# Three z units among the gate steps of a delta stage, its meta recurrence among the merge steps, and the input of the next up-projection rounded from the scaled tiles of a layer norm

## What is computed

```python
proj = h @ w_in                                   # k, q, v, z of 8 heads x 128, and two columns a head
qkv = silu(causal_dwconv(qkv, conv_w))            # then l2norm of q and k
m = where(strict, k_beta @ k.T * decay, 0)        # by chunk and head
a_mat = eye + m                                   # its inverse is applied to v and k
def step(state, inp):                             # over the chunks
    v_new = u_i - w_i @ state
    o_i = qg_i @ state + qk_i @ v_new
    state = state * exp(gl_i) + kd_i.T @ v_new
o = o * rsqrt(mean(o * o) + eps) * norm_w * silu(z)
```

## Time and profile before

| | |
|---|---|
| median of 3 runs | 1368.37 us (1367.38 to 1368.89) |
| the profiled execution | 1367.68 us, its span 1366.0 us |
| TensorE busy | 1298.6 us, 95% of the span |
| DVE, ACT, POOL busy | 1004.5, 688.7 and 45.0 us |
| DMA | 244.62 MB, mean 179 GB/s |
| granted TensorE clock, mean | 0.987 |

### The profile page before, as it was taken

The page is one execution under the profiler, slowest core; times in us unless marked ns, Lnnn a source line. Parts: engine busy times, 40 slices in busy tenths (PEclk is TensorE's granted clock), DMA queues, the critical chain, the costliest instruction groups (busy, mean ns, idle before and its releaser), DMA issues.

```text
span 1366.0 us, 29005 instructions
## 1 busy us (share of the span) xinstructions
PE 1298.6 (95%) x10514; PEld 1274.3 (93%) x10514; DVE 1004.5 (74%) x1811; ACT 688.7 (50%) x1098; POOL 45.0 (3%) x83
## 2 busy tenths in 40 slices
PE   6996999999999999999999799999999999999997
PEld 5995989899999999999999799999998989999997
DVE  6787654899897899899886677774565667777743
ACT  5863533465554354465554355553364554655531
POOL 0001000001001100000000000000000000000000
PEclk9998999999999999999999999999999999999999
DMA  6441002368888868668885346565455334556651
GB/s 222 142 152 47 1 17 78 124 208 292 270 296 288 276 210 296 186 211 289 273 288 172 114 129 184 180 220 184 132 170 177 117 101 141 170 182 182 220 182 40
DMA packets 65351, 244.62 MB, mean 179 GB/s; under 512 B 7264, under 2 KB 9600, under 8 KB 65280
## 3 DMA queue, kind: packets, MB, share of 16 engines
q1 hardware_dynamic: 54624, 204.70, 45.6%
q0 software_dynamic: 10656, 38.93, 9.2%
HBM read 242.56 MB, written 1.05 MB: 178 GB/s over the span
## 4 chain that ended last, share of the span: by engine, by line
PE 74%; DVE 5%; ACT 1%; issue 1%; DVEq 0%; ACTq 0%
PE ps L1582 22%; PE ps L1583 22%; PE ps L1584 22%; PE ps L1597 1%; DVE wlo L374 1%; PE ps L1603 1%; PE ps L1598 1%; PE ps L1963 1%; PE ps L1965 1%; PE ps L1964 1%; DVE xb L1259 1%; DVE xb L1289 1%; PE ps L2075 1%; ACT whi L367 0%; PE ps L2053 0%
## 5 line engine op out<-in xcount | busy, mean ns | idle before, releaser
L1582 PE MATMUL ps<-hhi,whi 128*128 128x258 f32 (+4 forms) x2024 | 578.3, 286 | 9.1 <-DVE small L1491 2.6
L1583 PE MATMUL ps<-hlo,whi 128*128 128x258 f32 (+4 forms) x2024 | 573.9, 284 | 0.0
L1584 PE MATMUL ps<-hhi,wlo 128*128 128x258 f32 (+4 forms) x2024 | 573.4, 283 | 0.0
L367 ACT ACTIVATE whi<-raw 128x1024 fp32r<-128x1024 f32 (+1 forms) x360 | 399.7, 1113 | 301.1 <-PE ps L1584 280.2
L374 DVE TENSOR_TENSOR wlo<-raw,whi 128x1024 fp32r<-128x1024 f32 (+1 forms) x360 | 463.1, 1292 | 107.6 <-ACT whi L367 105.5
L1582 PEld LDWEIGHTS ps<-hhi,whi 128*128 128x128 f32 x2024 | 383.5, 189 | 11.2 <-issue 7.4
L1583 PEld LDWEIGHTS ps<-hlo,whi 128*128 128x128 f32 x2024 | 384.2, 190 | 0.5 <-issue 0.2
L1584 PEld LDWEIGHTS ps<-hhi,wlo 128*128 128x128 f32 x2024 | 384.4, 190 | 0.0
L1582 PE MATMUL ps<-ahi,whi 128*128 128x256 f32 (+2 forms) x768 | 216.9, 282 | 1.4 <-DVE alo L1347 1.4
L1583 PE MATMUL ps<-alo,whi 128*128 128x256 f32 (+2 forms) x768 | 216.3, 282 | 0.0
L1584 PE MATMUL ps<-ahi,wlo 128*128 128x256 f32 (+2 forms) x768 | 215.8, 281 | 0.0
(11 more groups left out here) (362 smaller groups left out, 1414.5 us busy)
## 6 DMA issues: line engine op xcount, KB each, us to landing
raw<-in_w_up SPq DMA_DIRECT2D x176, 512.0 KB, 4.2
raw<-in_w_down SPq DMA_DIRECT2D x64, 704.0 KB, 4.4
ring<-in_ada_w POOLq DMA_DIRECT2D x72, 512.0 KB, 5.0
raw<-in_w_mix SPq DMA_DIRECT2D x48, 512.0 KB, 3.6
raw<-in_w_a_in SPq DMA_DIRECT2D x32, 512.0 KB, 3.7
raw<-in_w_b_cx SPq DMA_DIRECT2D x16, 512.0 KB, 4.5
raw<-in_w_a_out SPq DMA_DIRECT2D x8, 512.0 KB, 3.6
raw<-in_w_b_gate SPq DMA_DIRECT2D x8, 512.0 KB, 4.7
```

What stands on the lines that cost most here:

```text
L367: nc.scalar.activation(whi[:, s, 0:blocks * P], raw[:, s, 0:blocks * P], ACT.Copy).then_inc(hi_split, 1)
L1582: nc.tensor.matmul(out, whi[:, s, w], rhi(k0 + k), start=first and k == 0, stop=False)
L1583: nc.tensor.matmul(out, whi[:, s, w], rlo(k0 + k), start=False, stop=False)
L1584: ins = nc.tensor.matmul(out, wlo[:, s, w], rhi(k0 + k), start=False, stop=last and k == blocks - 1)
```

## The change

1. `STEPS` is another order, with the four large gate groups first and the merges after them in the order of the groups; `ROWS_AT` and `ROWS` put the transposes of k first, and of v the meta block's first.
2. On TensorE z units 24, 25 and 26 (`one(U_Z + j)`) stand right behind `gate_mm` of the first three groups. ACT copies them raw into `zs` (`early_z`) and applies silu once, to all three, at step 14 (`late_silu`).
3. The convolution of v unit 23 on DVE moves behind `gate_diff(0)`, and its weight split with those of units 24 and 25 to steps 16, 18 and 21. ACT's silu of unit 23 moves to step 14, and a dummy exponential ahead of unit 23 brings the table load forward.
4. The meta block's products move to steps 24, 26 and 28 (`meta_v0`, `meta_s0`, `meta_o0`). The eight scaled copies of its values move from DVE to ACT (`meta_values`).
5. The chunk loop has units 27 to 30 between its products. The squares are taken in two parts, even blocks (with the meta block) before the last copies of the outputs, odd blocks behind them, and the sums follow in two parts; no unit stands between loop and sums.
6. DVE computes the modulation columns before the last down-projection (`down1`), with one column product more (`SHIFT_A`). In the last layer norm ACT writes `hhi[m]` from the scaled tile `xb[m]` itself, and `hf[m]` right behind it. `up2` begins with three slots, the mean of squares stands inside unit 3 behind its third block, and the split of slot 3 on DVE moves behind the eight `hlo` tiles. `IDLE_PRODUCTS[3]` goes from (3, 10) to (3, 4).

```diff
 STEPS = [
-    (0, 0), (0, 1), (1, 0), (0, 2), (0, 3), (1, 1), (2, 0), (1, 3), (1, 2), (0, 4), (2, 1), (3, 0), (2, 3), (2, 2), (1, 4), (3, 1),
...
+    (0, 0), (0, 1), (0, 2), (0, 3), (1, 0), (1, 1), (0, 4), (1, 2), (1, 3), (2, 0), (2, 1), (1, 4), (2, 2), (2, 3), (3, 0), (3, 1),
...
+LATE_SILU, META_V0, META_S0, META_O0 = 14, 24, 26, 28
+EARLY_Z = 3
+ODD_SUMS = 144
+LATE_SPLITS = {16: 0, 18: 1, 21: 2}
...
-IDLE_PRODUCTS = {0: (3, 4), 1: (3, 4), 2: (3, 4), 3: (3, 10), 5: (3, 4), 7: (0, 0)}
+IDLE_PRODUCTS = {0: (3, 4), 1: (3, 4), 2: (3, 4), 3: (3, 4), 5: (3, 4), 7: (0, 0)}
...
+            mine(nc.scalar.activation(small[:, 312:313], S_(7)[:, 0:1], ACT.Exp))
+            a_v(U_Z - 1)
...
+            def early_z(u):
+
+                act.wait_ge(unit_done, u + 1)
+                nc.scalar.activation(zs[:, u - U_Z, :], ps[u % SLOTS][:, TOK - N_A:TOK], ACT.Copy).then_inc(tiles_read, 1)
+                a_next_hi(u)
+
+            def late_silu():
+
+                a_silu(U_Z - 1, 1)
+                act.wait_ge(tiles_read, SLOTS + U_Z + EARLY_Z)
+                nc.scalar.activation(zs[:, 0:EARLY_Z, :], zs[:, 0:EARLY_Z, :], ACT.Silu)
+
+            def meta_values():
+
+                act.wait_ge(mm_v0, 1)
+                nc.scalar.activation(vn[:, 7, :], ps[4][:, 0:P], ACT.Copy).then_inc(v0_read, 1)
+                for h in range(HEADS):
+                    last = nc.scalar.activation(rr[:, h, :], ps[4][:, 0:P], ACT.Copy, scale=vec[:, V_HEAD + h:V_HEAD + h + 1])
+                last.then_inc(vm_ready, 1)
...
+                if c:
+                    act.wait_ge(o_read, 3)
+                    nc.scalar.activation(ex[:, MB, :], ot[:, MB, :], ACT.Square)
+                    nc.scalar.activation(ex[:, 0:MB:2, :], ot[:, 0:MB:2, :], ACT.Square).then_inc(sq_gdn, 1)
...
-            nc.scalar.activation(ex[:], ot[:], ACT.Square).then_inc(sq_gdn, 1)
-            a_z(U_Z + 6)
+            nc.scalar.activation(ex[:, 1:MB:2, :], ot[:, 1:MB:2, :], ACT.Square).then_inc(sq_gdn, 1)
...
+                if i == 3:
+                    nc.scalar.activation(hhi[:, :, SEQ:N_SH], shifts(0), ACT.Copy)
...
+                        if i == 3:
+                            nc.scalar.activation(hhi[:, m, 0:n], xb[:, m, 0:n], ACT.Identity, bias=small[:, SHIFT_A + m:SHIFT_A + m + 1],
+                                                 scale=a_of(0)(m)).then_inc(rhs_hi, 1)
                         nc.scalar.activation(hf[:, m, 0:n], xb[:, m, 0:n], ACT.Identity, bias=shift(m)).then_inc(hf_ready, 1)
...
+                if j == 0:
+                    conv(U_Z - 1, (U_Z - 1) % SLOTS)
                 if l == 0:
                     gate_products(g)
                 elif l:
                     mask_x((l, g))
...
+                if j in LATE_SPLITS:
+                    d_z(U_Z - 1 + LATE_SPLITS[j])
...
-            dve.wait_ge(v0_read, 1)
-            for h in range(HEADS):
-                last = nc.vector.tensor_scalar(rr[:, h, :], ps[4][:, 0:P], vec[:, V_HEAD + h:V_HEAD + h + 1], None, ALU.mult)
...
+            nc.vector.tensor_tensor(small[:, SHIFT_A:SHIFT_A + KT], small[:, 72:72 + KT], vec[:, V_LN + 7 * KT:V_LN + 8 * KT],
+                                    ALU.mult).then_inc(mods_ready, 1)
             dve.wait_ge(mods_ready, 1)
+            rest_of_splits = dve_residual(3, "down1", N_F1, N_B - N_F1)
+            dve_norm(3, N_F1, xb, LN_EPS, ln_gain(3), None,
+                     between=lambda: step(nc.vector.memset(sums[:, 0:SEQ], 0.0)))
...
-                ahead = 3 if version in ("gdn", "ln0", "ln1", "ln2", "rms1") else 2
+                ahead = 3 if version in ("gdn", "ln0", "ln1", "ln2", "rms0", "rms1") else 2
...
+                    unit(t, s, KT, n, lambda k: hhi[:, k, 0:n], lambda k: hlo[:, k, 0:n],
+                         k_wait=(lambda k: pe_norm(norm, SEQ) if k == 3 else None) if norm == 4 else None)
...
                     gate_mm(g)
+                    if j < EARLY_Z:
+                        one(U_Z + j)
...
+                if j == META_V0:
+                    meta_v0()
+                if j == META_S0:
+                    meta_s0()
+                if j == META_O0:
+                    meta_o0()
...
-            one(U_Z + 6)
...
+            for parity in range(2):
+                pe.wait_ge(o_read, 3 + 2 * parity)
+                pe.wait_ge(sq_gdn, U_V + 2 + parity)
+                for i, b in enumerate(range(parity, NBLK, 2)):
+                    last = token_sum(5, ex[:, b, :], ODD_SUMS * parity + i)
```

More of the change, by code:

```diff
@@ L692, in act_late_norm @@
             def act_late_norm(i, which, version, ready, squares, left):
-                for m in range(KT):
+                for m in range(KT if ready else 0):
                     ready(m)
@@ L1021, in _ @@
             nc.vector.scalar_tensor_tensor(S_(16), S_(12), -1.0, S_(9), ALU.mult, ALU.mult).then_inc(cols_ready, 1)
-            for u in range(U_V + 3, U_Z):
+            for u in range(U_V + 3, U_Z - 1):
                 d_v(u)
@@ L1114, in _ @@
             nn = small[:, 320:320 + NBLK]
-            step(nc.vector.tensor_tensor(nn, ps[7][:, 0:NBLK], S_(13), ALU.mult))
+            for parity in range(2):
+                at_, n = ODD_SUMS * parity, len(range(parity, NBLK, 2))
+                mine(nc.vector.tensor_tensor(nn[:, parity:NBLK:2], ps[5][:, at_:at_ + n], S_(13)[:, parity:NBLK:2], ALU.mult))
+            mine.after()
             step(nc.vector.tensor_tensor(nn, nn, S_(13), ALU.mult))
@@ L1354, in _ @@
             dve_hidden("up1", N_F1, V_FCONV + FT * 3)
-            rest_of_splits = dve_residual(3, "down1", N_F1, N_B - N_F1)
-            dve_ln(3, N_F1, splits=rest_of_splits)
-            MIX = PH["mix"]
-            M0 = MIX.first // SLOTS
-            def mix_splits(u, k=1):
-                for v in range(u, u + k):
-                    nxt = v + SLOTS
-                    split_lo(dve, M0 + nxt // SLOTS, nxt % SLOTS, KT)
-            step(nc.vector.memset(sums[:, 0:SEQ], 0.0))
             dve.wait_ge(ada_done, ADA_OPS)
@@ L1605, in first_step @@
                 for s in range(ahead, until):
-                    if s == {4: 3, 6: 2}.get(norm):
+                    if s == 2 and norm == 6:
                         pe_norm(norm, SEQ)
-                    unit(t, s, KT, n, lambda k: hhi[:, k, 0:n], lambda k: hlo[:, k, 0:n])
+                    unit(t, s, KT, n, lambda k: hhi[:, k, 0:n], lambda k: hlo[:, k, 0:n],
+                         k_wait=(lambda k: pe_norm(norm, SEQ) if k == 3 else None) if norm == 4 else None)
             def stream(phase, n, version=None, norm=None):
@@ L1656, in _, with token_sum @@
             v_b = lambda b: blocks_at(2, b, 1)
-            def token_sum(x, to):
-                return nc.tensor.matmul(ps[7][:, to:to + P], x, ones, start=True, stop=True)
+            def token_sum(bank, x, to):
+                return nc.tensor.matmul(ps[bank][:, to:to + P], x, ones, start=True, stop=True)
             one(U_V)
@@ L1744, in turn, with meta_v0, meta_s0, meta_o0 @@
                 last.then_inc(mm_turn, 1)
+            def meta_v0():
+                pe.wait_ge(gu_ready, MERGE_AT[3, 4] + 1)
+                pe.wait_ge(tr_read, ROWS.index((1, 4)) + 1)
+                nc.tensor.matmul(ps[4][:, 0:P], gu[:, MB, :], v_b(MB), start=True, stop=True).then_inc(mm_v0, 1)
+            def meta_s0():
+                pe.wait_ge(vm_ready, 1)
+                for q in range(2):
+                    nc.tensor.matmul(ps[5 - q][:, :], ktm[:, MB, :], rr[:, 4 * q:4 * q + 4, :], start=True, stop=True).then_inc(mm_s0, 1)
+            def meta_o0():
+                pe.wait_ge(v0_read, 1)
+                pe.wait_ge(s_ready, 1)
+                nc.tensor.matmul(ps[5][:, 0:P], vn[:, 7, :], ca[:, MB, :], start=True, stop=True).then_inc(mm_o0, 1)
             for j in range(len(STEPS) + 2):
@@ L1762, in _ @@
             pe.wait_ge(tr_read, len(ROWS_AT))
[L1763 to L1770 removed]
+            pe.wait_ge(o_read, 1)
             for c in range(2):
                 for q in range(2):
[L1773 removed]
+                    pe.wait_ge(s_ready, 2 * c + q + 1 if c else 2)
                     for j in range(4):
```

134 lines of the change are left out of this document (74 added, 60 removed).

## The result

The changed kernel takes 1350.55 us (median of 4 runs, 1347.68 to 1350.89) against 1368.63 of the kernel before (median of 4, 1367.38 to 1370.51): ratio 0.9862, 95% interval 0.9844 to 0.988. Forecast was 1351.5. The profiled execution has a span of 1348.9 us against 1366.0.

A forecast was written before the change was run, and what follows sets the result against it. TensorE, busy 95% of the span, was taken as the bound, so only idle time and low clock could be won. Delta stage 12.3 + seam 4.6 = 16.9 us off 1367.68 gives 1350.8, median 1351.5; range 1348.5 to 1357.0.

The forecast's parts named there:

- Second opening: Start of `gate_mm(1)`: forecast near 110.15 instead of 111.69, with TensorE waiting 1.7 us from 108.5.
- Three units fill the stage: Gates: DVE needs 6.05 us a group, TensorE 6.2; order ahead by 4.66 us, plus 9.3 us for three z units.
- Moved into the merges: Merges: three splits and late silu cost 0, bound 3.2 us; meta values 0.45 late, one-block gate 0.15.
- seam of the sums: Behind the chunk loop, between even and odd sums: 0.2 us lost, 1.9 without the cover of the even sums.
- Seam: From `down1` into `up2`: mean of squares 5.4 us earlier, less half of 1.6 for clock, gives 4.6 us.
- Clock: Low-clock loss behind new waits: 0.9 us behind the 3.0 us wait (bounds 0 and 1.7), half of 1.6 at the seam.
- delta stage: Gates, merges, chunk loop and sums: 4.66 + 9.3 - 0.45 - 0.15 - 0.2 - 0.9 = 12.3 us gained.
- 1 (covers fail): Four pieces in the merges and both clock stretches at their bounds: 4.9 us less gain, 1356.4 us; chance 0.2.
- rival 2: No stretch falls to the low clock and no seam shows: 0.9 + 0.8 + 0.35 more gain, 1349.5 us; chance 0.17.
- 3: Next unit of `up2` waits for something the earlier rounding doesn't move: seam gain 0, 1356.1 us; chance 0.06.
- 4: Clock falls in the 1.7 us wait at 108.5 and stays low; until 165 gives 6.2 us slower, 1374.6; chance 0.02.
- 5: Whole kernel: a small gain or none for a reason not seen; chance 0.05.

The follow-up runs named there:

- Experiment 2: Changed kernel with the three z units between the gate products cut to one block of eight: 1352.81 us, ratio 0.9895.
- the repetition: The changed kernel timed and profiled once more, unaltered: 1349.18 us, ratio 0.9854 to the kernel before.
- the halves: Kernel before with points 1 to 5 alone: 1353.72 us, ratio 0.9902; with point 6 alone: 1362.64 us, ratio 0.9974.

## Why the prediction was right

Point by point, by its own steps (measured behind `gate_mm(0)` unless said):

- **Second opening**: forecast 7.45 us and a wait of 1.7; measured 7.46 and 1.62. The forecast counted the 0.32 us for the tap, but not that the dummy brings it: without it the opening stands at 7.06. The table load again took 1.28 us, and by the 2.7 us of the Trainium skill, ScalarE: Activation LUTs, Rules for kernel authors, it would have been 8.9: the trace decides for 1.28.
- **Three units fill the stage**: right. 6.18 and 6.11 us a group against 6.05 to 6.2; turn(0,3) at 27.14 against 27.4, its waits 0.32 and 2.69 against 0.4 and 3.0. Experiment 2 shows that the units cost nothing there.
- **Moved into the merges**: splits and late silu 0, as said. Behind a merge of the one-block group TensorE waits 0.21 (164.12), which the prediction hasn't. Meta values 0.18 us instead of 0.45, one-block gate 0.20 instead of 0.15, seam of the sums 0.1 instead of 0.2 (4.05 us for 17 sums against 3.96).
- **Seam**: first product of `up2` 7.0 us closer to `down1`, as said; mean of squares 5.59 closer against 5.4; chain behind it 6.08 against 5.97; waits 1.21 and 3.58 against 2.1 and 3.8. ACT's two operations a tile take 0.89 us, forecast 0.82. The 5.59 holds the loss of 2.4 us that the kernel before had at the low clock from 783 to 791; it is in the 796.55 that the prediction started from, which doesn't name it.
- **Clock**: the term that was mis-sized and partly misplaced. The prediction took 0.9 behind turn(0,3) and 0.8 at the seam, with 1.6 as the upper bound there. Nine profiles have the wait of 2.7 us ahead of turn(0,3) unfilled, and five of them have a low stretch at it, with losses of 1.4 to 3.1. Behind the short waits at the end of the merges, to which the prediction gave nothing since before they stood at clock 1.00, three of the eight profiles of the new order that have them have one of 1.6 to 1.7. Behind the 3.58 us wait all seven profiles that have it do, five with 2.7 to 3.0 and two with 1.7: all over the bound, two by only 0.1. The means are 1.2, 0.6 and 2.5, in all 4.3 us where 1.7 was forecast.
- **Why the sum still came out**: partly by chance. In the two profiles the delta stage shows a lead of 11.4 (12.28 less 0.86) for 12.3, the seam 5.59 - 0.11 - 2.48 = 3.0 for 4.6, together 14.4 for 16.9; the start-up, 0.4 between sums and `down1`, and the low stretch that only before met at 1142 gave 0.86 + 0.41 + 1.47 = 2.7 back. Over more executions the change is worth a little more than forecast: the medians differ by 18.1 and, in the repetition, 19.0, and the halves by 13.6 and 4.7 for 12.3 and 4.6, although the clock took 2.6 us more than forecast in the mean of the profiles. What made up for it in the medians is not shown. It may lie in the low stretches of the kernel before, whose executions run at a mean clock of 0.985 to 0.991 against 0.991 to 0.994 of the changed one, or in waits like the one at 457.56; there is one profile of the kernel before.

The Trainium skill, TensorE: Matmul & The Clock Gate, What's actually happening, makes both new waits suspect, since the throttled state is the default. By the sum of the prediction both stretches then cost their full 1.7 and 1.6 (its 1353.2 should be 1353.1 by these terms); at the seam the clock fell each time and cost more, at turn(0,3) it fell in five of nine.

Of the rivals, 1 (covers fail) fell for the covers and held for the clock's share, 1.2 and 2.5 in the mean against bounds of 1.7 and 1.6. The 1349.5 of rival 2 is as near the two medians, 1350.55 and 1349.18, as the forecast, but its reason, no low stretch, did not hold: luck. 3, 4 and 5 did not occur. What stays open: whether filling waits is worth anything on average. At the merges it took no time off the median, where a stretch stands in only three of eight profiles anyway, and with all the waits filled the ratio was that of the changed kernel.

## What to carry to other kernels

Work that waits for nothing belongs into the stage where the bounding engine waits for a chain on another, measured by that chain's length per step (here 6.05 us against 2.65 + 3.10 + 0.44); it pays its own length and saves the low clock that the waits would bring (experiment 2). Where one operation must stand in a critical chain, put it where the chain waits anyway: the convolution between difference and products hid 0.70 us besides. Better still, take out what need not stand there: the split that left the chain was worth 1.14. When a wait is shortened by pulling its chain forward, look at how the cover is spread: the one long wait of 3.6 us cost 1.7 to 3.0 more in clock in all seven profiles. With unit 3 put behind the mean of squares the same chain cost nothing in one profile and 1.7 in the two others, and its restart came 1.13 us earlier in two of the three.

## What the runs showed of the hardware

- Low stretches come by chance: the same kernel has them behind different waits in different executions. At each beyond the start-up stands idle time of TensorE, from 6.86 us down to waits of 0.87 and 0.78 in a row, or of 1.14 and 0.44. Most lose 1.4 to 1.7 us, the others 2.2 to 3.1.
- How often one comes differs from wait to wait. Three waits of 2.58, 2.08 and 1.80 us, at 1032, 1126 and 1149 in the changed kernel, stand in all 14 profiles, that of before among them; a low stretch follows them in 12, 8 and 3. It followed 3.58 in seven of seven and 2.7 in five of nine, and the waits of 1.36 to 1.45 us between 240 and 560 in none.
- By an estimate they make most of the spread between executions: the spans of the kernel before go from 1362.1 us at a mean clock of 0.991 to 1371.0 at 0.985, those of the changed one from 1345.4 at 0.994 to 1349.2 at 0.992. 0.006 of 1366 us is 8.2 of the 8.9 us between the first two, 0.002 of 1347 is 2.7 of 3.8.
- On ACT, an operation on 128x256 with both scale and bias from a column takes longer than one with the bias alone (0.59 to 0.60 us against 0.49 to 0.50). Rows of both in the changed kernel:

```profile
765.20 0.60 ACT L742 ACTIVATE hhi<-xb,small 128x256 fp32r<-128x256 f32 x1 [2.10 <-DVE xb L1344]
765.71 0.49 ACT L744 ACTIVATE hf<-xb,vec 128x256 f32<-128x256 f32 x1
766.11 0.59 ACT L742 ACTIVATE hhi<-xb,small 128x256 fp32r<-128x256 f32 x1
```

The two together take 0.91 from start to start here and 0.89 from the second pair on, where 0.82 was assumed for twice the shorter one. The type of the output is not the reason: the eight `hhi` of the kernel before, fp32r too but with the scale alone from a column, took 3.29 us, 0.41 each.
